# Kernel of two pairs of transformer blocks: order of work at the edges of the feed-forward sublayers

## The chip, the cores and the metric

One program on one core of a Trainium2 chip. The metric is the device time of one execution in microseconds. A core has four engines that compute (TensorE, VectorE, ScalarE, GpSimdE) and a fifth, SyncE, that issues transfers here. The engines run side by side and wait for each other by semaphores. In the trace they are PE (matrix multiplications; PEld for its weight loads), DVE, ACT, POOL and SP.

## The reference

256 tokens of width 1024 pass two layers of a first block and two layers of a second. A layer has three sublayers: feed-forward, mixer, feed-forward. The first block's sublayers read a condition (shift, scale, gate); the second block's take a norm of the result too.

```python
# first block, one layer
hn = _modulate(_rms_norm(h, norm_g[l, 0]), sh1, sc1)      # xn * (1 + scale) + shift
h = h + 0.5 * g1[:, None, :] * _swiglu(hn, ffn1_w_in[l], ffn1_w_out[l])
...                                                        # mixer: four kinds side by side, h = h + g2 * (mixed @ w_out)
hn = _modulate(_rms_norm(h, norm_g[l, 2]), sh3, sc3)
h = h + 0.5 * g3[:, None, :] * _swiglu(hn, ffn2_w_in[l], ffn2_w_out[l])

# second block
h = rms_norm(x, gn[0])
x = x + 0.5 * rms_norm(swiglu(h, w_ffn1_gate[l], w_ffn1_up[l], w_ffn1_down[l]), gn[1])

def _swiglu(x, w_in, w_out):
    gate, up = jnp.split(x @ w_in, 2, axis=-1)
    return (jax.nn.silu(gate) * up) @ w_out                # width 2816
```

## The kernel before

The twelve sublayers are numbered n = 0 to 11; n = 1, 4, 7, 10 are mixers and the other eight are feed-forward. Tokens are in two blocks of 128, a = 0 and 1. `h` holds the running sum in fp32. Every fp32 product is made of three multiplications: an operand is split into a high part, which ScalarE makes by a copy to a shorter format, and a low part, which VectorE makes by subtracting the high part from the original; low x high, high x low and high x high are added up in PSUM. `tok3` (lines 539 to 541) is this triple.

Weights come in units of 1 MB through three buffers: SyncE loads `raw`, ScalarE's `hi` (line 1049) makes `whi`, VectorE's `lo` (line 1507) makes `wlo`. Unit k can be loaded once unit k-3 has its low part. A feed-forward sublayer works through the 2816 hidden columns in eleven groups of 256. A group is two gate/up units (each half of the 1024 input columns) and one down unit. `k0` and `k0 + 1` are the sublayer's first two units.

At a boundary between sublayers the work on a token block a is a chain. VectorE adds the result to h (`residual`, lines 1526 and 1527), or, after sublayers of the second block, ScalarE squares the result first (line 1068) and VectorE scales by its norm. ScalarE squares h (line 1057), VectorE finds the inverse root (`norm_root`, lines 1422 to 1427) and scales h into `xs`, half by half (`scale_x`: lines 1568 and 1569 with norm_g and shift for n < 6, line 1572 after that). TensorE turns each half into PSUM banks 6 and 7 (`turn_x`, line 588), ScalarE copies it to `xh` (`upper_x`, line 1074) and VectorE subtracts to `xl` (`lower_x`, line 1578). In VectorE's order (`boundary`) block 0 comes first, then block 1's residual, then the low part of unit k0 + 1, then block 1.

TensorE's order at a feed-forward entry is written out in `ffn`: both halves of block 0 turned, 12 multiplications with unit k0, block 1's first half turned, 12 with unit k0 + 1, block 1's second half turned, four multiplications that zero the accumulators, then 24 multiplications for block 1. The groups follow. At the first one TensorE waits for the low part of unit k0 + 2 and for `h32`, the product of VectorE (lines 1652 and 1654). ScalarE makes the high part of that unit after its last `upper_x`.

At the end of the sublayer the last group's hidden values of both blocks are turned together into bank 6 (line 611), copied (line 1147) and subtracted (line 1659) as one tile of 512 columns, and lie in `xh` and `xl` from then on. All orders are program order on each engine; no scheduler moves anything.

## Time and profile before

| | us |
|---|---|
| median of 3 runs | 2605.33 (2604.96 to 2612.98) |
| the profiled execution | 2607.96 |
| its span in the profile | 2606.1 |
| TensorE busy | 2312.9 (89%) |
| VectorE busy | 1640.0 (63%) |
| ScalarE busy | 1082.2 (42%) |
| GpSimdE busy | 117.8 (5%) |
| mean granted TensorE clock | 0.941 |

Times in the rows are microseconds from the span's start. A row of the timeline has start, duration, engine, line and operation, what is written and read, and how many were merged; the bracket is how long the engine was idle before it and what ended that. Matrix multiplications are pipelined, so the difference of two starts is what one costs, not its own duration. In a view by stretches every engine has its busy time and its count, then come TensorE's granted clock, the DMA engines' busy share and what they moved in GB/s. The clock is 1.00 for 2.4 GHz and 0.50 for 1.2 GHz.

### The profile page before, as it was taken

To read this page: it belongs to the slowest core of one execution; us is meant where nothing else is said; L and a number is where in the kernel's file an instruction comes from. 1 tells how busy PE (TensorE), PEld (TensorE's weight loads), DVE (VectorE), ACT (ScalarE), POOL (GpSimd) and SP (SyncE) were. 2 spreads that over 40 slices of the span, in tenths; PEclk is the share of its full clock that TensorE was granted. 3 is DMA by queue.
4 is the path that set the end of the run, shared out by engine and by line. 5 is a ranking of instruction groups with operands and counts; after the bars stand their busy time and mean duration, and the time that the engine had idled before them with its cause. 6 is when DMAs were issued, how large, how long until landed. Compare 5 with 4: busy or idle time off the path is not lost.

```text
span 2606.1 us, 31632 instructions
## 1 busy us (share of the span) xinstructions
PE 2312.9 (89%) x11730; PEld 1941.2 (74%) x11740; DVE 1640.0 (63%) x1933; ACT 1082.2 (42%) x1246; POOL 117.8 (5%) x176
## 2 busy tenths in 40 slices
PE   1999799999899799899899787789989978957998
PEld 0787786787687686688788687668868868946887
DVE  6786875776776784655655566565565565646555
ACT  2434454343343363434343454434434335434443
POOL 1000033000000023000000000000000000000000
PEclk9999999999999998999999898789989989968999
DMA  7796552685586553456455442335546544323553
GB/s 241 269 314 199 194 170 81 242 284 192 203 280 220 166 197 97 152 187 194 161 191 182 136 121 80 113 129 194 188 134 195 191 145 130 117 61 115 185 185 113
DMA packets 321186, 452.75 MB, mean 174 GB/s; under 512 B 32470, under 2 KB 269896, under 8 KB 320072
## 3 DMA queue, kind: packets, MB, share of 16 engines
q1 hardware_dynamic: 314224, 439.43, 51.6%
q0 software_dynamic: 2816, 9.51, 1.1%
q10 hardware_dynamic: 4056, 2.58, 0.4%
q8 instruction: 59, 0.97, 0.2%
q14 instruction: 31, 0.25, 0.0%
HBM read 450.43 MB, written 1.05 MB: 173 GB/s over the span
## 4 chain that ended last, share of the span: by engine, by line
PE 78%; DVE 13%; ACT 4%; issue 2%; POOL 1%; DMA 1%; ACTq 1%; DVEq 0%; SPq 0%
PE ps L539 19%; PE ps L541 19%; PE ps L540 19%; PE ps L532 4%; PE ps L533 4%; PE ps L534 4%; PE ps L917 2%; PE ps L611 1%; DVE wlo L1507 1%; PE ps L756 1%; POOL nrm L2082 1%; PE ps L588 1%; DMA arena<-in_ada_w_dram 1%; PE ps L704 1%; PE ps L569 1%
## 5 line engine op out<-in xcount | busy, mean ns | idle before, releaser
L1507 DVE TENSOR_TENSOR wlo<-raw,whi 128x2048 fp32r<-128x2048 f32 (+1 forms) x348 | 791.7, 2278 | 439.8 <-ACT whi L1049 439.6
L1049 ACT ACTIVATE whi<-raw 128x2048 fp32r<-128x2048 f32 x346 | 659.6, 1909 | 275.2 <-PE ps L541 247.6
L539 PE MATMUL ps<-whi,xl 128*128 128x512 f32 x1600 | 657.8, 411 | 19.4 <-DVE xl L1866 10.5
L540 PE MATMUL ps<-wlo,xh 128*128 128x512 f32 x1600 | 635.3, 397 | 0.0
L541 PE MATMUL ps<-whi,xh 128*128 128x512 f32 x1600 | 634.7, 397 | 0.0
L539 PEld LDWEIGHTS ps<-whi,xl 128*128 128x128 f32 x1600 | 308.4, 193 | 91.1 <-issue 13.9
L541 PEld LDWEIGHTS ps<-whi,xh 128*128 128x128 f32 x1600 | 307.6, 192 | 67.4
L540 PEld LDWEIGHTS ps<-wlo,xh 128*128 128x128 f32 x1600 | 308.4, 193 | 65.4 <-issue 4.8
L532 PE MATMUL ps<-xl,whi 128*128 128x256 f32 x896 | 264.5, 295 | 16.5 <-DVE wlo L1507 15.2
L533 PE MATMUL ps<-xh,wlo 128*128 128x256 f32 x896 | 259.6, 290 | 0.0
L534 PE MATMUL ps<-xh,whi 128*128 128x256 f32 x896 | 259.1, 289 | 0.0
L539 PE MATMUL ps<-whi,hidl 128*128 128x512 f32 x640 | 252.5, 395 | 0.0
L540 PE MATMUL ps<-wlo,hidh 128*128 128x512 f32 x640 | 249.4, 390 | 0.0
L541 PE MATMUL ps<-whi,hidh 128*128 128x512 f32 x640 | 249.3, 390 | 0.0
L532 PEld LDWEIGHTS ps<-xl,whi 128*128 128x128 f32 x896 | 178.3, 199 | 20.6 <-DVE wlo L1507 16.0
L533 PEld LDWEIGHTS ps<-xh,wlo 128*128 128x128 f32 x896 | 178.3, 199 | 0.6 <-issue 0.5
L534 PEld LDWEIGHTS ps<-xh,whi 128*128 128x128 f32 x896 | 178.0, 199 | 0.0
L1142 ACT ACTIVATE sq<-ps 128x256 f32<-128x256 f32 x176 | 67.5, 384 | 246.8 <-PE ps L541 246.8
L1637 DVE SCALAR_TENSOR_TENSOR arena<-arena,condT 128x1024 f32<-128x1024 f32 x120 | 154.5, 1288 | 23.3 <-DMA arena<-in_ada_w_dram 21.8
L1150 ACT ACTIVATE hidh<-ps 128x512 fp32r<-128x512 f32 x80 | 47.9, 599 | 283.0 <-PE ps L611 283.0
L1662 DVE TENSOR_TENSOR hidl<-ps,hidh 128x512 fp32r<-128x512 f32 x80 | 55.3, 691 | 140.9 <-ACT hidh L1150 140.9
L540 PEld LDWEIGHTS ps<-wlo,hidh 128*128 128x128 f32 x640 | 120.3, 188 | 25.9 <-issue 1.4
(332 smaller groups left out, 2340.3 us busy)
## 6 DMA issues: line engine op xcount, KB each, us to landing
raw<-in_ffn_w_in_dram SPq DMA_DIRECT2D x176, 512.0 KB
arena<-in_ada_w_dram SPq DMA_DIRECT2D x128, 512.0 KB, 5.7
raw<-in_w_in_dram SPq DMA_DIRECT2D x54, 1024.0 KB
raw<-in_ffn_w_out_dram SPq DMA_DIRECT2D x44, 1024.0 KB
raw<-in_w_ffn_gate_dram SPq DMA_DIRECT2D x88, 512.0 KB
raw<-in_w_ffn_up_dram SPq DMA_DIRECT2D x88, 512.0 KB
raw<-in_w_ffn_down_dram SPq DMA_DIRECT2D x44, 1024.0 KB
raw<-in_w_out_dram SPq DMA_DIRECT2D x16, 1024.0 KB
```

The source lines that it names most:

```text
L532: pe.matmul(o, wh, al, start=start, stop=False, **kw)
L533: pe.matmul(o, wl, ah, start=False, stop=False, **kw)
L534: return pe.matmul(o, wh, ah, start=False, stop=stop, **kw)
L539: pe.matmul(o, al, wh, start=start, stop=False, **kw)
L540: pe.matmul(o, ah, wl, start=False, stop=False, **kw)
L541: return pe.matmul(o, ah, wh, start=False, stop=stop, **kw)
L917: pe.matmul(ps[:, PVB, ch * S:ch * S + S], diag[d % RING], ypad[:, ch, tap:tap + S], start=(tap == 0), stop=(tap == CONVK - 1)).then_inc(d ...
L1049: act.activation(whi[:, k % 3, :], raw[:, k % 3, :], ACT.Copy).then_inc(hi_done, 1)
L1142: act.activation(sig[:, a, :], ps[:, a, 0:256], ACT.Sigmoid).then_inc(sig_ready, 1)
L1507: tt(a[0], a[1], a[2].bitcast(F32), ALU.subtract).then_inc(lo_done, 1)
L1637: stt(seg, adam[:, at, :], scalar, seg, ALU.mult, ALU.add).then_inc(adam_used, 1)
L1662: tt(hidl[:, :, :].rearrange("p f t -> p (f t)"), ps[:, HT, :], hidh[:, :, :].bitcast(F32).rearrange("p f t -> p (f t)"), ALU.subtract).th ...
```

## The change

Four edits.
1. The last group's hidden values are turned, copied and subtracted by token block, block 0 into bank 6 and block 1 into bank 7 (`turn_last`, `upper_last`, `lower_last`), with semaphores of their own. The last down unit of block 0 needs block 0's part only. ScalarE's high part of the next sublayer's first unit comes between its two copies, VectorE's low part between its two subtractions. Bank 7 also carries the modulation's sums, so TensorE waits for the reads of these.
2. For n < 6 h is multiplied with norm_g (times 1 + scale) ahead of the inverse root (`gained`); behind it one operation multiplies with the root and adds the shift. For the first half of each block `gained` is issued ahead of the root, for the second between the two scalings.
3. The first use of x by TensorE is split (`gate_up_first`): eight multiplications that read `xh` alone are issued when it is there, the four with `xl` later.
4. The turns of x are spread: the second half of block 0 after the first eight multiplications, block 1's first half after unit k0 + 1's 12, its second half after eight of block 1.

```diff
+                def gate_up_first(k, a, half, part):
+
+                    wh, wl = as4(whi, k % 3), as4(wlo, k % 3)
+                    t = slice(a * P, a * P + P)
+                    pe.wait_ge((xh_ready, x_ready)[part], 4 * n + 2 * a + half + 1)
+                    for q in range(4):
+                        kc = 4 * half + q
+                        if part == 0:
+                            pe.matmul(ps[:, a, :], xh[:, kc, t], wl[:, q, :], start=(kc == 0), stop=False)
+                            ins = pe.matmul(ps[:, a, :], xh[:, kc, t], wh[:, q, :], start=False, stop=False)
+                        else:
+                            ins = pe.matmul(ps[:, a, :], xl[:, kc, t], wh[:, q, :], start=False, stop=(kc == KC - 1))
+                    return ins
+
+                def turn_last(a):
+
+                    pe.wait_ge(h32_ready, 2 * (g0 + GROUPS - 1) + a + 1)
+                    for f in range(2):
+                        ins = pe.transpose(ps[:, HT + a, f * P:f * P + P],
+                                           hid32[:, a, f * P:f * P + P], ident[:, :])
+                    ins.then_inc(tail_turned, 1)
 
...
                 turn_x(n, 0, 0)
+                split_ready(L, k0)
+                gate_up_first(k0, 0, 0, 0)
                 turn_x(n, 0, 1)
-                split_ready(L, k0)
-                gate_up(k0, 0, 0, True)
+                gate_up_first(k0, 0, 0, 1)
+                split_ready(L, k0 + 1)
+                gate_up_first(k0 + 1, 0, 1, 0)
+                gate_up_first(k0 + 1, 0, 1, 1).then_inc(gu_ready, 1)
                 turn_x(n, 1, 0)
-                split_ready(L, k0 + 1)
-                gate_up(k0 + 1, 0, 1, True).then_inc(gu_ready, 1)
-                turn_x(n, 1, 1)
                 for b in range(4):
                     pe.matmul(ps[:, ACC + b, :], zerow[:, 0:P], zerow[:, :], start=True, stop=True,
                               skip_group_check=True)
-                gate_up(k0, 1, 0, True).then_inc(unit_used, 1)
-                gate_up(k0 + 1, 1, 1, True).then_inc(unit_used, 1)
+                gate_up_first(k0, 1, 0, 0)
+                turn_x(n, 1, 1)
+                gate_up_first(k0, 1, 0, 1).then_inc(unit_used, 1)
+                gate_up_first(k0 + 1, 1, 1, 0)
+                gate_up_first(k0 + 1, 1, 1, 1).then_inc(unit_used, 1)
...
                 k += 7
-                down(k, 0)
-                turn_hid(GROUPS - 1)
-                down(k, 1, (0,))
+                down(k, 0, (0,))
+                turn_last(0)
+                down(k, 0, (1,))
+                if m:
+                    pe.wait_ge(mod_read, SUMS[m] + 6)
+                if n == 0:
+                    pe.wait_ge(gate0_read, 2)
+                turn_last(1)
                 split_ready(L, k + 1)
-                pe.wait_ge(hid_ready, g0 + GROUPS)
+                pe.wait_ge(tail_hid, 2 * L.ffn(j) + 1)
                 down(k + 1, 0, last=True).then_inc(acc_done, 1)
-                down(k, 1, (1,)).then_inc(unit_used, 1)
+                down(k, 1).then_inc(unit_used, 1)
+                pe.wait_ge(tail_hid, 2 * L.ffn(j) + 2)
                 down(k + 1, 1, last=True).then_inc(unit_used, 1)
...
+                def upper_last(a):
+                    act.wait_ge(tail_turned, 2 * L.ffn(j) + a + 1)
+                    act.activation(lasth[:, 2 * a:2 * a + 2, :],
+                                   ps[:, HT + a, 0:S].rearrange("p (c t) -> p c t", c=2),
+                                   ACT.Copy).then_inc(tail_hidh, 1)
 
...
                 sigmoid(g + 2, 1, k + 6)
+                upper_last(0)
                 if n < SUBS - 1:
                     hi(L, k + 9)
-                upper(g + 2)
+                upper_last(1)
...
+            def gained(n, a, f):
+
+                c = slice(512 * f, 512 * f + 512)
+                return tt(xs[:, a, c], h[:, a, c], gain[:, c], ALU.mult)
+
             def scale_x(n, a, f):
 
                 o = xs[:, a, 512 * f:512 * f + 512]
                 c = slice(512 * f, 512 * f + 512)
                 r = rstat[:, a, 1:2]
                 if n < 6:
-                    st(stt(o, h[:, a, c], r, gain[:, c], ALU.mult, ALU.mult))
-                    tt(o, o, shift[:, c], ALU.add).then_inc(xs_ready, 1)
+                    if f:
+                        st(gained(n, a, f))
+                    stt(o, o, r, shift[:, c], ALU.mult, ALU.add).then_inc(xs_ready, 1)
...
-                norm_root(n, 0)
                 if n < 6:
                     dve.wait_ge(mod_read, SUMS[n] + 6)
+                    gained(n, 0, 0)
                 else:
                     dve.wait_ge(gate_loaded, 16 * (n - 5))
+                norm_root(n, 0)
                 scale_x(n, 0, 0)
                 scale_x(n, 0, 1)
                 lower_x(n, 0, 0)
                 lower_x(n, 0, 1)
                 finish(n - 1, 1)
                 lo(L, k0 + 1)
+                if n < 6:
+                    gained(n, 1, 0)
                 norm_root(n, 1)
                 scale_x(n, 1, 0)
...
+                def lower_last(a):
+                    dve.wait_ge(tail_hidh, 2 * L.ffn(j) + a + 1)
+                    c = slice(2 * a, 2 * a + 2)
+                    tt(lastl[:, c, :], ps[:, HT + a, 0:S].rearrange("p (c t) -> p c t", c=2),
+                       lasth[:, c, :].bitcast(F32), ALU.subtract).then_inc(tail_hid, 1)
 
...
-                lower(g + 2)
+                lower_last(0)
                 if n < SUBS - 1:
                     lo(L, k + 9)
+                lower_last(1)
```

Three places where instructions move, all around the entry of sublayer 2 or the end of a feed-forward sublayer. A row is line, operation, what is written and read, shape, and the semaphores waited for; "..." leaves out rows that repeat.

TensorE at a feed-forward entry, before. `ps<-ident,u` is a turn of x, `whi` and `wlo` are the weight unit's parts; the last row is the first group's first multiplication:

```order
L588 MATMUL ps<-ident,u 128x128 [waits xs_ready]
L588 MATMUL ps<-ident,u 128x128 [waits xs_ready]
...
L539 MATMUL ps<-whi,xl 128x512 [waits x_ready,lo_done]
...
L588 MATMUL ps<-ident,u 128x128 [waits x_ready,xs_ready]
...
L539 MATMUL ps<-whi,xl 128x512 [waits x_ready,lo_done]
...
L588 MATMUL ps<-ident,u 128x128 [waits x_ready,xs_ready]
...
L638 MATMUL ps<-zerow 128x512 x4
L539 MATMUL ps<-whi,xl 128x512 [waits x_ready]
...
L539 MATMUL ps<-whi,xl 128x512 [waits x_ready]
...
L539 MATMUL ps<-whi,xl 128x512 [waits h32_ready]
```

and now:

```order
L589 MATMUL ps<-ident,u 128x128 [waits xs_ready]
...
L614 MATMUL ps<-wlo,xh 128x512 [waits xh_ready,lo_done]
...
L589 MATMUL ps<-ident,u 128x128 [waits xs_ready]
...
L617 MATMUL ps<-whi,xl 128x512 [waits x_ready]
...
L614 MATMUL ps<-wlo,xh 128x512 [waits xh_ready,lo_done]
...
L589 MATMUL ps<-ident,u 128x128 [waits x_ready,xs_ready]
...
L660 MATMUL ps<-zerow 128x512 x4
L614 MATMUL ps<-wlo,xh 128x512 [waits xh_ready]
...
L589 MATMUL ps<-ident,u 128x128 [waits x_ready,xs_ready]
...
L617 MATMUL ps<-whi,xl 128x512 [waits x_ready]
...
L614 MATMUL ps<-wlo,xh 128x512 [waits xh_ready]
...
L540 MATMUL ps<-whi,xl 128x512 [waits h32_ready]
```

The second turn moved behind the first unit's eight multiplications with xh, the third behind the second unit's 12, and behind the fourth stand 16 multiplications where 24 stood.

TensorE at the end of a feed-forward sublayer, before. The rows of line 539 that read `hidl` belong to the last but one group's down unit, those that read `xl` to the last group's:

```order
L539 MATMUL ps<-whi,hidl 128x512 [waits hid_ready,lo_done]
...
L611 MATMUL ps<-ident,u 128x128 [waits h32_ready]
L611 MATMUL ps<-ident,u 128x128 x3
L539 MATMUL ps<-whi,hidl 128x512
...
L539 MATMUL ps<-whi,xl 128x512 [waits hid_ready,lo_done]
...
L539 MATMUL ps<-whi,hidl 128x512
...
L539 MATMUL ps<-whi,xl 128x512
```

and now:

```order
L540 MATMUL ps<-whi,hidl 128x512 [waits hid_ready,lo_done]
...
L624 MATMUL ps<-ident,u 128x128 [waits h32_ready]
L624 MATMUL ps<-ident,u 128x128
L540 MATMUL ps<-whi,hidl 128x512
...
L624 MATMUL ps<-ident,u 128x128 [waits h32_ready,mod_read]
...
L540 MATMUL ps<-whi,xl 128x512 [waits tail_hid,lo_done]
...
L540 MATMUL ps<-whi,hidl 128x512
...
L540 MATMUL ps<-whi,xl 128x512 [waits tail_hid]
```

Four turns at one place became two and two, and block 0's last product has six multiplications fewer ahead of it; they stand behind it.

VectorE at the entry of sublayer 2, before. `rstat` is the root, `u` holds xs, `wlo` is the low part of unit k0 + 1:

```order
L1527 TENSOR_TENSOR h<-h,sq 128x512 [waits dve_step]
L1422 SCALAR_TENSOR_TENSOR rstat<-ssq 128x1 [waits sq_ready]
...
L1568 SCALAR_TENSOR_TENSOR u<-h,rstat,gain 128x512 [waits mod_read,dve_step]
L1569 TENSOR_TENSOR u<-u,shift 128x512 [waits dve_step]
L1568 SCALAR_TENSOR_TENSOR u<-h,rstat,gain 128x512
L1569 TENSOR_TENSOR u<-u,shift 128x512 [waits dve_step]
L1578 TENSOR_TENSOR xl<-ps,xh 128x4x128 [waits xh_ready] x2
...
L1527 TENSOR_TENSOR h<-h,sq 128x512 [waits dve_step]
L1507 TENSOR_TENSOR wlo<-raw,whi 128x2048 [waits hi_done]
L1422 SCALAR_TENSOR_TENSOR rstat<-ssq 128x1 [waits sq_ready]
```

and now:

```order
L1561 TENSOR_TENSOR h<-h,sq 128x512 [waits dve_step]
L1599 TENSOR_TENSOR u<-h,gain 128x512 [waits mod_read]
L1456 SCALAR_TENSOR_TENSOR rstat<-ssq 128x1 [waits sq_ready]
...
L1609 SCALAR_TENSOR_TENSOR u<-u,rstat,shift 128x512 [waits dve_step]
L1599 TENSOR_TENSOR u<-h,gain 128x512
L1609 SCALAR_TENSOR_TENSOR u<-u,rstat,shift 128x512 [waits dve_step]
L1618 TENSOR_TENSOR xl<-ps,xh 128x4x128 [waits xh_ready] x2
...
L1561 TENSOR_TENSOR h<-h,sq 128x512 [waits dve_step]
L1541 TENSOR_TENSOR wlo<-raw,whi 128x2048 [waits hi_done]
L1599 TENSOR_TENSOR u<-h,gain 128x512
L1456 SCALAR_TENSOR_TENSOR rstat<-ssq 128x1 [waits sq_ready]
```

One product with the gain moved ahead of each root; behind the root one operation is left for the first half, and two for the second as before.

## Rows read from the trace of the kernel before

**Rows 1.** Page; stretch: busy (count) of PE, PEld, DVE, ACT, POOL, clock, DMA, GB/s
```profile
PE 2312.9 (89%) x11730; PEld 1941.2 (74%) x11740; DVE 1640.0 (63%) x1933; ACT 1082.2 (42%) x1246; POOL 117.8 (5%) x176
...
690.00:860.00 170.00, 169.89 (x757) 138.03 (x756) 119.53 (x108) 69.42 (x64) 3.16 (x2) 1.00 0.75 256
```

**Rows 2.** Timeline (start, duration, engine, line), the last group of sublayer 2
```profile
644.03 0.39 PE L539 MATMUL ps<-whi,hidl 128*128 128x512 f32 x1
...
644.51 1.91 ACT L1049 ACTIVATE whi<-raw 128x2048 fp32r<-128x2048 f32 x1
...
646.75 0.60 PE L611 MATMUL ps<-ident,u 128*128 128x128 f32 x4
...
648.62 2.28 DVE L1507 TENSOR_TENSOR wlo<-raw,whi 128x2048 fp32r<-128x2048 f32 x1
...
648.86 0.47 PE L539 MATMUL ps<-whi,xl 128*128 128x512 f32 x1
...
651.90 0.69 DVE L1526 TENSOR_TENSOR sq<-ps,gate 128x512 f32<-128x512 f32 x1 [0.99 <-PE ps L541]
```

**Rows 3.** Timeline, the entry of sublayer 3, up to its first group
```profile
655.44 0.16 DVE L1422 SCALAR_TENSOR_TENSOR rstat<-ssq 128x1 f32<-128x1 f32 x1 [0.79 <-ACT sq L1057]
...
657.23 0.75 DVE L1568 SCALAR_TENSOR_TENSOR u<-h,rstat,gain 128x512 f32<-128x512 f32 x1
...
658.76 0.33 PE L588 MATMUL ps<-ident,u 128*128 128x128 f32 x1 [2.82 <-DVE u L1569]
...
661.93 0.69 DVE L1578 TENSOR_TENSOR xl<-ps,xh 128x512 fp32r<-128x512 f32 x1 [1.16 <-ACT xh L1074]
...
665.19 2.29 DVE L1507 TENSOR_TENSOR wlo<-raw,whi 128x2048 fp32r<-128x2048 f32 x1
...
670.71 0.69 PE L588 MATMUL ps<-ident,u 128*128 128x128 f32 x2 [5.80 <-DVE u L1569]
...
676.74 0.60 PE L588 MATMUL ps<-ident,u 128*128 128x128 f32 x4
...
677.08 0.64 PEld L638 LDWEIGHTS ps<-zerow 128*128 128x128 bf16 x4
...
677.38 0.60 ACT L1074 ACTIVATE xh<-ps 128x512 fp32r<-128x512 f32 x1 [4.92 <-PE ps L588]
...
677.86 0.58 PE L539 MATMUL ps<-whi,xl 128*128 128x512 f32 x1
...
677.88 1.91 ACT L1049 ACTIVATE whi<-raw 128x2048 fp32r<-128x2048 f32 x1
...
682.48 0.42 DVE L1654 TENSOR_TENSOR u<-sq,ps 128x256 f32<-128x256 f32 x1
```

**Rows 4.** Timeline, TensorE at the first turn of sublayer 2
```profile
451.69 1.12 PE L588 MATMUL ps<-ident,u 128*128 128x128 f32 x4 [3.31 <-DVE u L1569]
```

**Rows 5.** Timeline, sublayer 9: first square, first turn, second lowering
```profile
1917.28 0.60 ACT L1068 ACTIVATE sq<-ps 128x512 f32<-128x512 f32 x1 [3.91 <-PE ps L541]
...
1926.04 1.97 PE L588 MATMUL ps<-ident,u 128*128 128x128 f32 x8 [4.72 <-DVE u L1572]
...
1928.67 0.69 DVE L1578 TENSOR_TENSOR xl<-ps,xh 128x512 fp32r<-128x512 f32 x1 [0.16 <-ACT xh L1074]
```

**Rows 6.** Timeline, sublayer 11: first turn, both lowerings
```profile
2399.20 1.32 PE L588 MATMUL ps<-ident,u 128*128 128x128 f32 x8 [3.37 <-DVE u L1572]
...
2400.53 1.35 DVE L1578 TENSOR_TENSOR xl<-ps,xh 128x512 fp32r<-128x512 f32 x2 [0.71 <-ACT xh L1074]
```

**Rows 7.** Columns as in rows 1, entries of 3, 11, 6; timeline, turn of 6
```profile
660.00:663.00 3.00, 2.85 (x9) 2.45 (x10) 1.84 (x4) 0.65 (x2) 0.00 (x0) 0.50 0.00 0
2401.00:2406.00 5.00, 4.63 (x11) 3.70 (x12) 4.65 (x15) 0.35 (x2) 0.00 (x0) 0.50 0.00 0
1256.00:1259.00 3.00, 2.90 (x12) 2.05 (x12) 2.93 (x6) 0.72 (x2) 0.00 (x0) 1.00 0.00 0
...
1253.74 0.99 PE L588 MATMUL ps<-ident,u 128*128 128x128 f32 x5 [2.09 <-DVE u L1572]
```

More of the change, by code:

```diff
@@ L214, in program @@
         ht_done, hidh_ready, hid_ready = sem("ht_done"), sem("hidh_ready"), sem("hid_ready")
+        tail_turned, tail_hidh, tail_hid = sem("tail_turned"), sem("tail_hidh"), sem("tail_hid")
         diag_ready, diag_used = sem("diag_ready"), sem("diag_used")
@@ L592, in ffn, with gate_up @@
             def ffn(L, n, j, k0):
-                g0, m = L.ffn(j) * GROUPS, (n + 1 if n < 5 else 0)
-                def gate_up(k, a, half, first=False):
+                g0, h0, m = L.ffn(j) * GROUPS, L.ffn(j) * (GROUPS - 1), (n + 1 if n < 5 else 0)
+                def gate_up(k, a, half):
                     wh, wl = as4(whi, k % 3), as4(wlo, k % 3)
                     t = slice(a * P, a * P + P)
-                    if first:
-                        pe.wait_ge(x_ready, 4 * n + 2 * a + half + 1)
                     for q in range(4):
@@ L621, in down @@
                         if last:
-                            ah, al = lasth[:, 2 * f + a, :], lastl[:, 2 * f + a, :]
+                            ah, al = lasth[:, 2 * a + f, :], lastl[:, 2 * a + f, :]
                         for b in range(2):
@@ L662, in group @@
                     split_ready(L, k + 4, ki)
-                    pe.wait_ge(hid_ready, g0 + g + 1)
+                    pe.wait_ge(hid_ready, h0 + g + 1)
                     if last:
@@ L1134, in ffn @@
             def ffn(L, n, j, k0):
-                g0, m = L.ffn(j) * GROUPS, (n + 1 if n < 5 else 0)
+                g0, h0, m = L.ffn(j) * GROUPS, L.ffn(j) * (GROUPS - 1), (n + 1 if n < 5 else 0)
                 def sigmoid(g, a, k=0, i=0):
@@ L1144, in upper @@
                 def upper(g):
-                    act.wait_ge(ht_done, g0 + g + 1)
-                    if isinstance(g, int) and g == GROUPS - 1:
-                        act.activation(lasth, ps[:, HT, :].rearrange("p (c t) -> p c t", c=4),
-                                       ACT.Copy).then_inc(hidh_ready, 1)
-                    else:
-                        act.activation(hidh[:, :, :].rearrange("p f t -> p (f t)"), ps[:, HT, :],
-                                       ACT.Copy).then_inc(hidh_ready, 1)
+                    act.wait_ge(ht_done, h0 + g + 1)
+                    act.activation(hidh[:, :, :].rearrange("p f t -> p (f t)"), ps[:, HT, :],
+                                   ACT.Copy).then_inc(hidh_ready, 1)
+                def upper_last(a):
[3 more added lines that the diff above has]
+                                   ACT.Copy).then_inc(tail_hidh, 1)
                 hi(L, k0 + 2)
@@ L1618, in first @@
                 dve.wait_ge(mod_read, 4)
+                st(gained(0, 0, 0))
                 scale_x(0, 0, 0)
                 scale_x(0, 0, 1)
+                st(gained(0, 1, 0))
                 scale_x(0, 1, 0)
@@ L1646, in ffn @@
             def ffn(L, n, j, k0):
-                g0, m = L.ffn(j) * GROUPS, (n + 1 if n < 5 else 0)
+                g0, h0, m = L.ffn(j) * GROUPS, L.ffn(j) * (GROUPS - 1), (n + 1 if n < 5 else 0)
                 def product(g, a):
@@ L1656, in lower @@
                 def lower(g):
-                    dve.wait_ge(hidh_ready, g0 + g + 1)
-                    if isinstance(g, int) and g == GROUPS - 1:
-                        tt(lastl, ps[:, HT, :].rearrange("p (c t) -> p c t", c=4), lasth.bitcast(F32),
-                           ALU.subtract).then_inc(hid_ready, 1)
-                    else:
-                        tt(hidl[:, :, :].rearrange("p f t -> p (f t)"), ps[:, HT, :],
-                           hidh[:, :, :].bitcast(F32).rearrange("p f t -> p (f t)"), ALU.subtract).then_inc(hid_ready, 1)
+                    dve.wait_ge(hidh_ready, h0 + g + 1)
+                    tt(hidl[:, :, :].rearrange("p f t -> p (f t)"), ps[:, HT, :],
+                       hidh[:, :, :].bitcast(F32).rearrange("p f t -> p (f t)"), ALU.subtract).then_inc(hid_ready, 1)
+                def lower_last(a):
[3 more added lines that the diff above has]
+                       lasth[:, c, :].bitcast(F32), ALU.subtract).then_inc(tail_hid, 1)
                 lo(L, k0 + 2)
```

## The prediction

> **What bounds the kernel.** I read the page's first part, then the wait lists and a search of TensorE's idle time over the span, then the timeline around the sublayer boundaries. The reader is to see three things. First, TensorE is busy 89% of the span, and inside a feed-forward sublayer it is never idle: 169.89 of 170 us at full clock, VectorE 70% busy beside it [rows 1]. So nothing inside absorbs a delay or turns a gain into idle time: what the change does at a boundary is kept, whatever its sign. Second, at a boundary TensorE is idle twice. At the entry of sublayer 3 that is 2.82 us before the first turn of x and 5.80 us before the third, both ended by VectorE [rows 3]. Third, between these waits TensorE runs at half rate: granted 0.50, 11 multiplications of 512 columns in 4.63 us (0.42 to 0.43 each), against 1.00 and 0.225 us each in the interior, 170 us by 757 instructions [rows 1, 7]. I number sublayers 0 to 11; 0, 2, 3, 5, 6, 8, 9, 11 are feed-forward, and 1 to 5 have the shift and the scaled norm_g.
>
> **Last group by token block.** Before, a block's last products follow 12 multiplications, four turns, 6 more multiplications, then the wait for `lastl`; first issue at 648.86, VectorE's residual at 651.90 [rows 2]. Now six multiplications from 644.03 (1.36 us), two turns, six, two turns, and the last 12 start at 647.15 if block 0's high and low parts are there. They are: turn issued at 645.4, ScalarE's copy from 645.9 (0.64 us behind the turns, as at 676.74, less for half of them), 0.4 us, VectorE 0.4 us, done 646.7. So block 0's sums are complete 1.7 us earlier, 650.2. For these half-size copies and subtractions no row stands; 0.60 and 0.69 of the whole ones bound them above, half of that below; I take 0.4, as the 256-column product in rows 3 takes 0.42. ScalarE's split of the next unit (1.91 us) moves from 644.51 behind the first copy, 646.2 to 648.1; VectorE's lower part of it then runs 648.1 to 650.4, and the second block's subtraction ends at 650.7. VectorE is thus free at 650.7, not 650.2: where it reads the sums itself (sublayers 1, 3, 4, 6) the gain is 1.2 us. Where ScalarE squares the sums first (7, 9, 10; it waits for TensorE [rows 5]) it is the full 1.7. At the program's end the second block's own sums come only 0.3 earlier, and VectorE 0.8.
>
> **norm_g ahead of the root.** The first product h x gain (0.69) goes into VectorE's 0.79 us wait for the squares [rows 3]: free; if the squares were there already it would cost up to 0.69. Behind the root one operation of 0.75 remains of 0.75 + 0.69 (the scaling at 657.23, and a two-operand operation as at 651.90): first turn 0.7 us earlier, in sublayers 1 to 5. For block 1 VectorE doesn't wait, so the product only changes places: nothing gained.
>
> **First turn, in sum:** 1.9 earlier in 1, 3, 4; 0.7 in 2, 5; 1.2 in 6; 1.7 in 7, 9, 10; 0 in 8, 11. In the mixers (1, 4, 7, 10) PE's order is untouched and every later wait is VectorE's chain, which moves along: -(1.9+1.9+1.7+1.7) = -7.2 us. End: -0.8.
>
> **High part first.** Eight multiplications now stand between the turns of x's halves. They start when ScalarE has copied the first half: turn + 0.69 + 0.60 + 0.05 = 1.34 us. At 0.23 they take 1.8, at 0.43 3.4 (3.2 if the clock returns within). Then turn 2, 0.69 (1.1 at half rate) to ScalarE, 0.63 to VectorE. So the second lowering starts 4.5 us after the first turn at full clock, 6.3 at half. Before it was 3.2 us in 3 [rows 3], which I take for 2 and 5 too, 2.6 in 9 [rows 5] and 2.0 in 11 (1.35 us for both, from 2400.53) [rows 6]. Queued behind this lowering in VectorE are block 1's residual, the lower half of the second gate/up unit, the root and block 1's scaling: all of that moves.
>
> **Second turn later.** Before, TensorE resumed when root and scaling were done, 670.71, 3.23 us after the split of the second unit ended (665.19 + 2.29) [rows 3]. Now the next 12 multiplications need only that split: 3.2 us off the wait, 2.5 where no shift is added (from 6 on). Resume, against before:
> 2 and 5, half rate: -3.2 - 0.7 + (6.3 - 3.2) = -0.8 each;
> 3, full: -3.2 - 1.9 + (4.5 - 3.2) = -3.8;
> 6, full: -2.5 - 1.2 + (4.5 - 2.0) = -1.2;
> 9, half: -2.5 - 1.7 + (6.3 - 2.6) = -0.5;
> 8 and 11, half: -2.5 + (6.3 - 2.0) = +1.8 each.
> Sum -3.5. Which clock I take: the idle time before the first turn, 2.82 us in 3 and 3.31 to 4.72 in 2, 9 and 11, left it at half rate [rows 3 to 7]; in 6, after 2.09, it stayed full [rows 7]. In 3 and 6 that idle time shrinks to about 1.4 and 1.2.
>
> **What comes late next.** This is the largest term. Before, the fourth turn (676.74) was issued ahead of the zeroing and 24 multiplications: 0.34 + 0.78 + 24 x 0.225 = 6.5 us to the first group. The chain behind it is turn, ScalarE's copy (677.38), the split of the third unit in ScalarE's queue (677.88), its lower part, the product, which ends at 682.90 [rows 3]: 6.16 us, hidden with 0.3 to spare. Now only 16 multiplications follow the fourth turn: 0.34 + 3.6 = 3.94 us. The chain is as long, since ScalarE and VectorE still have copy, split, lower and product in that order. With 0.05 us for the signal TensorE waits 6.21 - 3.94 = 2.25 us ahead of the first group. Against it stands that one turn now runs at full instead of half rate (0.4, of which the multiplications in its place take back 0.2 or all). Net 2.0 in each of seven: +14. Its bounds: 1.8 (sublayer 3, all 12 of the resume at half rate) and 2.3. Loads follow the lower parts and move with TensorE; DMA at 0.75 in the interior [rows 1] leaves room.
> Sublayer 0: eight multiplications slip into a wait that is not in my rows' pattern and the same late chain is paid: 0, bounds -2 and +2.
> No multiplication is added; waits on banks 6 and 7 (the modulation's copies) are for work that ScalarE has long done: 0, and at most one copy, 0.6, in the five sublayers that have them.
>
> **Sum:** -7.2 - 0.8 - 3.5 + 14 + 0 = +2.5 us on the profiled execution's 2607.96 (its span 2606.1 and 1.9 around it). That execution lies 2.6 above the median of 2605.33; on the median: 2607.8.
>
> On the clock: in sublayer 6 the trace shows 2.09 us idle and still 1.00 [rows 7], in 3 a longer one and 0.50. [...]
>
> **Rivals.**
> 1. Slower: the new stall of 2.25 us, just above the 2.09 that kept the clock and below the 2.82 that did not, drops TensorE to half rate at the first group. Ten to twelve multiplications at 0.43 for 0.23 cost 2.0 to 2.4. It decides from an idle time between 2.1 and 2.8. Seven times 2.0: +16.5, 2621.8. Against: full work stands on both sides of the stall, where at a boundary there are only turns. Chance 0.16.
> 2. Half rate at every first half: +6.1, 2611.4. Chance 0.17.
> 3. Full rate at every first half, since TensorE starts sooner after its turns: 2, 5, 8, 9, 11 gain 1.8 each, -9: sum -6.5, 2598.8. Against: 8 and 11 wait 3.4 us as before. Chance 0.10.
> 4. The late chain hides after all (a split of the third unit that ran ahead of the copy, or a slower TensorE in front of it): -14, sum -11.5, 2593.8. For it: half-rate multiplications behind the fourth turn would cover it. Against: by then TensorE has worked through 20 multiplications without a wait, and both queues run in program order. Chance 0.12.
> My forecast 0.45.
>
> A measurement of this kernel tells 0.3% (7.8 us) from no change. Faster: rival 4 and a quarter of 3: 0.15. Slower: rival 1, a third of 2, a tenth of mine: 0.26. Same: 0.59. Range: from 2597, between rivals 4 and 3, to 2621, near rival 1.
>
> **What would show it.** In the new trace: TensorE's last 12 for block 0 about 1.7 us after the first two turns, with no wait; VectorE's residual 1.2 us sooner; first turn of 3 idle-free except for 1.4 us. The third turn without idle time and the idle time moved to the high-part multiplication of the second unit, waiting for VectorE's lower split. An idle time of 2 to 2.3 us at the first group's first multiplication in seven sublayers, ended by the product: the step I would be most wrong without. Second lowering 4.5 or 6.3 us after the first turn, as the clock is. I am wrong if that idle time is absent, if it is over 3 us, or if the interior shows idle time at all.

## The result and the profile after

The kernel after takes 2623.8 us (median of 7 runs, 2616.8 to 2631.8), the kernel before on the same chip 2606.1: ratio 1.0064 [1.0053, 1.0075], 17.7 us slower. The forecast was 2607.8, range 2597 to 2621. The profiled executions differ by 17.1 (spans 2623.2 and 2606.1).

The page of the kernel after, first part, and its interior of sublayer 3 (stretch, busy and count of PE, PEld, DVE, ACT, POOL, clock, DMA, GB/s), which answer to [rows 1]:

```profile
PE 2316.9 (88%) x11730; PEld 1940.6 (74%) x11740; DVE 1639.2 (62%) x1941; ACT 1082.8 (41%) x1254; POOL 115.1 (4%) x176
...
690.00:860.00 170.00, 170.00 (x759) 138.26 (x758) 119.35 (x107) 69.53 (x65) 3.16 (x2) 1.00 0.77 263
```

The same number of matrix instructions, and an interior as full and as fast as before: the time was lost at boundaries alone.

The end of sublayer 2 and the first turn of sublayer 3 after (timeline: start, duration, engine, line, operation), which answer to [rows 2] and the head of [rows 3]:

```profile
651.30 0.39 ACT L1182 ACTIVATE xh<-ps 128x256 fp32r<-128x256 f32 x1 [1.20 <-PE ps L624]
...
651.72 0.43 DVE L1709 TENSOR_TENSOR xl<-ps,xh 128x256 fp32r<-128x256 f32 x1 [0.70 <-ACT xh L1182]
...
655.74 0.42 DVE L1709 TENSOR_TENSOR xl<-ps,xh 128x256 fp32r<-128x256 f32 x1
...
656.07 0.68 DVE L1560 TENSOR_TENSOR sq<-ps,gate 128x512 f32<-128x512 f32 x1
...
658.72 0.68 DVE L1599 TENSOR_TENSOR u<-h,gain 128x512 f32<-128x512 f32 x1
...
661.38 0.75 DVE L1609 SCALAR_TENSOR_TENSOR u<-u,rstat,shift 128x512 f32<-128x512 f32 x1
...
662.19 0.66 PE L589 MATMUL ps<-ident,u 128*128 128x128 f32 x4 [1.09 <-DVE u L1609]
```

Copy and subtraction of half size take 0.39 and 0.43 (I took 0.4 each), VectorE goes straight from the subtraction to the residual, the product with norm_g lies ahead of the root, and from the residual to the first turn it is 6.12 us instead of 6.86. TensorE is idle for 1.09 us there, not 2.82. This half of the change does what it should.

The entry of sublayer 3 after, same columns, which answers to the rest of [rows 3]. L614 and L615 are the multiplications that read `xh`, L617 those with `xl`, L589 the turns:

```profile
663.63 0.47 PE L614 MATMUL ps<-wlo,xh 128*128 128x512 f32 x1 [0.78 <-ACT xh L1105]
...
666.67 1.05 PE L589 MATMUL ps<-ident,u 128*128 128x128 f32 x4
...
668.39 0.69 DVE L1618 TENSOR_TENSOR xl<-ps,xh 128x512 fp32r<-128x512 f32 x1 [4.18 <-ACT xh L1105]
...
671.65 2.28 DVE L1541 TENSOR_TENSOR wlo<-raw,whi 128x2048 fp32r<-128x2048 f32 x1
...
673.99 0.80 PE L614 MATMUL ps<-wlo,xh 128*128 128x512 f32 x1 [5.33 <-DVE wlo L1541]
...
678.64 0.60 PE L589 MATMUL ps<-ident,u 128*128 128x128 f32 x4
...
681.88 0.60 PE L589 MATMUL ps<-ident,u 128*128 128x128 f32 x4
...
682.52 0.60 ACT L1105 ACTIVATE xh<-ps 128x512 fp32r<-128x512 f32 x1 [2.64 <-PE ps L589]
...
683.01 1.91 ACT L1080 ACTIVATE whi<-raw 128x2048 fp32r<-128x2048 f32 x1
...
684.95 2.29 DVE L1541 TENSOR_TENSOR wlo<-raw,whi 128x2048 fp32r<-128x2048 f32 x1 [1.11 <-ACT whi L1080]
...
687.61 0.42 DVE L1699 TENSOR_TENSOR u<-sq,ps 128x256 f32<-128x256 f32 x1
...
688.09 0.50 PE L540 MATMUL ps<-whi,xl 128*128 128x512 f32 x1 [1.89 <-DVE u L1699]
```

Read it from the bottom. The first group's first multiplication waits 1.89 us for the product, and the product ends a chain that began with the fourth turn at 681.88: turn, copy, split, lower part, product, without a pause in it. Further up, the second turn is issued at 666.67, so VectorE waits 4.18 us for its second lowering (6.20 us after the first turn), while TensorE's next 12 multiplications need the lower split queued behind that lowering and wait 5.33 us.

What that comes to over the whole program, in the groups of the kernel after by line (busy, mean ns | idle time before them, what ended it):

```profile
L540 PE MATMUL ps<-whi,xl 128*128 128x512 f32 x1472 | 598.3, 406 | 25.6 <-DVE u L1699 15.1 <-DVE xl L1914 10.5
...
L614 PE MATMUL ps<-wlo,xh 128*128 128x512 f32 x128 | 65.7, 513 | 49.1 <-DVE wlo L1541 42.9 <-ACT xh L1105 6.2
...
L589 PE MATMUL ps<-ident,u 128*128 128x128 f32 x192 | 34.8, 317 | 53.6 <-DVE u L1612 39.9 <-DVE u L1609 13.7
```

And the turns' own group before:

```profile
L588 PE MATMUL ps<-ident,u 128*128 128x128 f32 x192 | 39.6, 349 | 100.8 <-DVE u L1572 62.8 <-DVE u L1569 37.9
```

47.2 us of idle time ahead of turns went away; 49.1 came at L614 and 15.1 at the group's first multiplication, eight times 1.89. I looked next for the clock behind these eight waits. Stretches of 3.5 us in the kernel after, each beginning 0 to 0.5 us behind the first multiplication after the wait (the fourth, at 1080.50, 1.1 us behind it, where the clock falls), columns as in rows 1:

```profile
83.75:87.25 3.50, 3.50 (x9) 2.72 (x10) 3.47 (x4) 2.34 (x2) 0.00 (x0) 0.53 0.82 249
479.75:483.25 3.50, 3.50 (x9) 2.74 (x10) 3.47 (x4) 2.12 (x2) 0.00 (x0) 0.52 0.89 253
688.10:691.60 3.50, 3.50 (x15) 2.91 (x16) 3.47 (x4) 2.13 (x2) 0.00 (x0) 1.00 0.71 228
1080.50:1084.00 3.50, 3.50 (x10) 2.76 (x9) 3.50 (x2) 1.04 (x1) 0.00 (x0) 0.52 0.90 281
1282.30:1285.80 3.50, 3.50 (x15) 2.90 (x16) 3.46 (x4) 2.11 (x2) 0.00 (x0) 1.00 0.85 255
1756.25:1759.75 3.50, 3.50 (x9) 2.78 (x10) 3.47 (x4) 2.02 (x2) 0.00 (x0) 0.53 0.83 260
1964.50:1968.00 3.50, 3.50 (x10) 2.70 (x10) 3.50 (x3) 1.63 (x1) 0.00 (x0) 0.53 0.88 293
2439.00:2442.50 3.50, 3.50 (x10) 2.67 (x10) 3.47 (x4) 1.86 (x2) 0.00 (x0) 0.52 0.92 285
```

In six of eight the granted clock is near 0.50 and 9 or 10 multiplications are issued; in sublayers 3 and 6 it stays at 1.00 and 15 are. The loss is counted best from the first multiplication after the wait to the turn that follows 24 of them, here in sublayers 3 and 2:

```profile
688.09 0.50 PE L540 MATMUL ps<-whi,xl 128*128 128x512 f32 x1 [1.89 <-DVE u L1699]
...
693.66 0.60 PE L632 MATMUL ps<-ident,u 128*128 128x128 f32 x4
```
```profile
479.73 0.67 PE L540 MATMUL ps<-whi,xl 128*128 128x512 f32 x1 [1.89 <-DVE u L1699]
...
486.88 0.49 PE L632 MATMUL ps<-ident,u 128*128 128x128 f32 x3
```

It is 5.58 us in 3 and 6, where the clock held, and 7.15 to 7.20 in the other six: 1.6 us lost at each, 9.7 in all.

### The profile page after: what moved, and what is told of

Read it like the earlier page. It is cut to its first block, busy times and chain, and to the rows that moved or that the text cites. A ratio compares the mean times of both kernels' runs of the same rounds, so it can differ in the third digit from the quotient of the medians.

```text
span 2623.2 us, 31648 instructions
## 1 busy us (share of the span) xinstructions
PE 2316.9 (88%) x11730; PEld 1940.6 (74%) x11740; DVE 1639.2 (62%) x1941; ACT 1082.8 (41%) x1254; POOL 115.1 (4%) x176
## 4 chain that ended last, share of the span: by engine, by line
PE 77%; DVE 13%; ACT 4%; issue 2%; POOL 1%; DMA 1%; ACTq 1%; DVEq 0%; SPq 0%
PE ps L540 18%; PE ps L542 17%; PE ps L541 17%; PE ps L533 4%; PE ps L534 4%; PE ps L535 4%; DVE wlo L1541 2%; PE ps L948 2%; PE ps L614 1%; PE ps L632 1%; PE ps L787 1%; PE ps L615 1%; POOL nrm L2130 1%; ACT whi L1080 1%; DMA arena<-in_ada_w_dram 1%
## 5 line engine op out<-in xcount | busy, mean ns | idle before, releaser
L540 PE MATMUL ps<-whi,xl 128*128 128x512 f32 x1472 | 598.3, 406 | 25.6 <-DVE u L1699 15.1
L541 PE MATMUL ps<-wlo,xh 128*128 128x512 f32 x1472 | 579.7, 394 | 0.0
L542 PE MATMUL ps<-whi,xh 128*128 128x512 f32 x1472 | 579.7, 394 | 0.0
L540 PEld LDWEIGHTS ps<-whi,xl 128*128 128x128 f32 x1472 | 280.1, 190 | 89.7 <-DVE u L1699 18.5
L542 PEld LDWEIGHTS ps<-whi,xh 128*128 128x128 f32 x1472 | 279.9, 190 | 61.1
L541 PEld LDWEIGHTS ps<-wlo,xh 128*128 128x128 f32 x1472 | 280.2, 190 | 60.0 <-issue 4.8
L540 PEld LDWEIGHTS ps<-whi,hidl 128*128 128x128 f32 x640 | 120.2, 188 | 25.9 <-issue 1.4
```

What stands on the lines that cost most here:

```text
L540: pe.matmul(o, al, wh, start=start, stop=False, **kw)
L541: pe.matmul(o, ah, wl, start=False, stop=False, **kw)
L542: return pe.matmul(o, ah, wh, start=False, stop=stop, **kw)
```

## The experiments

Each is compared with the kernel before on its own chip. "Against after" below is the quotient of the two ratios to before, times 2606.

**The fourth turn early (`fourth_early`), the second turn early (`second_early`), both.** Edits of the kernel after; `both_early` makes both and leaves only the third turn late.

```diff
                 turn_x(n, 0, 0)
+                turn_x(n, 0, 1)              # second_early
                 split_ready(L, k0)
                 gate_up_first(k0, 0, 0, 0)
-                turn_x(n, 0, 1)
...
+                turn_x(n, 1, 1)              # fourth_early
                 gate_up_first(k0, 1, 0, 0)
-                turn_x(n, 1, 1)
```

> The changed kernel with one line moved: block 1's second turn stands right behind the zeroing instead of behind eight multiplications of block 1. Theory (late chain and clock): the 1.89 us wait ahead of the first group goes in all eight sublayers (to 0.4 us at most, since 24 multiplications, 5.4 us, then stand behind the turn and the chain is 6.2 us), and with it the six stretches at half rate behind it, 1.5 us each. Together 8 x 1.5 to 1.9 + 6 x 1.5 = 21 to 24 us faster than the changed kernel, so 4 to 7 us faster than the kernel before (ratio about 0.998). Rival (the wait is a symptom; TensorE would be late for another reason, for instance the third unit's split itself): the wait moves elsewhere and the time stays within 5 us of the changed kernel, ratio 1.005 to 1.006.

> The changed kernel with the turn of block 0's second half back in front of the first eight multiplications. The fourth turn stays late. Theory: the second lowering comes 2.0 to 3.2 us after the first turn instead of 4.6 to 7.2 (1.9 to 4.2 us earlier in seven sublayers, 25 us in sum), and block 1's residual, the split of the second unit and the third turn all move with it; 25 us faster than the changed kernel, 8 us faster than before (ratio 0.997). The 1.89 us wait ahead of the first group stays in all eight. Rival (the eight multiplications only fill time that VectorE needs anyway): under 8 us faster than the changed kernel.

> Both turns moved as in the two other kernels: second turn ahead of the first eight multiplications, fourth right behind the zeroing. Only the third turn stays behind the second unit's 12. Theory: both gains add, 45 us faster than the changed kernel and about 28 us faster than before (ratio 0.989). Rival: they overlap, since either leaves TensorE waiting for VectorE; then no better than the better of the two, ratio 0.996 to 0.998.

Measured: 2596.5, 0.9960 [0.9947, 0.9973]; 2597.0, 0.9957 [0.9944, 0.9969]; 2569.8, 0.9854 [0.9839, 0.9868]. Against after -27, -28 and -54: the two late turns cost the same, and the costs add up. Groups of `both_early`:

```profile
L540 PE MATMUL ps<-whi,xl 128*128 128x512 f32 x1472 | 594.6, 404 | 11.6 <-DVE xl L1914 10.5 <-DVE u L1699 0.3
...
L614 PE MATMUL ps<-wlo,xh 128*128 128x512 f32 x128 | 62.0, 485 | 22.3 <-DVE wlo L1541 22.1
```

The wait for the product falls from 15.1 to 0.3 and that at L614 from 49.1 to 22.3. These 42 us of idle time explain most of the 54. The clock behind the first group's start holds in all eight sublayers (24 multiplications in 5.58 to 5.62 us), which is the 9.7 us from above; the last 3 us are not accounted for. All three came out better than expected (21 to 24, 25 and 45 us).

In `second_early` the wait of 1.89 us stays in all eight sublayers, and the clock fell behind it in seven: also in 3 and 6, where it had held in the kernel after, and not in sublayer 0, where it had fallen.

**The wait filled (`late_filled`).** The kernel after, with eight multiplications by zero added onto the output banks ahead of the first group; this separates the wait from the clock behind it.

```diff
                 gate_up_first(k0 + 1, 1, 1, 1).then_inc(unit_used, 1)
+                for b in range(8):
+                    pe.matmul(ps[:, ACC + b % 4, :], zerow[:, 0:P], zerow[:, :], start=False, stop=False,
+                              skip_group_check=True)
```

> The changed kernel with eight more multiplications by zero (512 columns, added onto the accumulators, result unchanged) ahead of the first group, that is in the 1.89 us wait; each takes about 0.2 us, 1.7 together. Theory (the wait's own time and the clock behind it are two separate costs): the wait's time stays, but TensorE is not idle, the clock doesn't fall there, and the six half-rate stretches of 1.5 us go: 9 us faster than the changed kernel, 8 to 9 slower than before (ratio 1.003). Rival (the clock falls for an earlier idle time, not for this one): no faster than the changed kernel, ratio 1.006 or a little above.

Measured: 2614.2, 1.0026 [1.0017, 1.0035], -10 against after, although the product comes no sooner. The traced execution took 2622.4, 8 over this median, so I read from it the stretches behind the zeros and not its whole. The zeros of sublayer 3 in the timeline, and then, for the six sublayers whose clock fell before, the window behind the zeros (stretch, PE busy and count, clock, DMA, GB/s):

```profile
681.79 1.90 PE L668 MATMUL ps<-zerow 128*128 128x512 bf16 x8
...
683.84 0.50 PE L540 MATMUL ps<-whi,xl 128*128 128x512 f32 x1
```
```profile
83.96:87.46 3.50, 3.50 (x15) 1.00 0.83 224
478.70:482.20 3.50, 3.50 (x15) 1.00 0.80 227
...
1079.59:1083.09 3.50, 3.50 (x15) 1.00 0.80 247
...
1755.22:1758.72 3.50, 3.50 (x15) 1.00 0.79 245
1962.71:1966.21 3.50, 3.50 (x15) 1.00 0.83 254
2437.76:2441.26 3.50, 3.50 (x15) 1.00 0.80 238
```

The six places that were at 0.52 are at 1.00, and 15 multiplications stand where 9 or 10 stood. The 24 multiplications behind the zeros take 5.58 to 5.62 us in all eight sublayers. So the fall of the clock is caused by the idle time and costs 10 us by itself, beside the 15 of the wait; the run (-10) and the count in the trace of the kernel after (9.7) agree.

**The parts apart.** `entry_only`: the kernel before with parts 3 and 4 of the change alone, TensorE's new order. `tail_and_gain`: the kernel after with the old order. `tail_only`: the last group by token block alone (part 1). `gain_only`: norm_g ahead of the root alone (part 2).

```diff
# tail_and_gain, from the kernel after; entry_only is the reverse, from the kernel before
                 turn_x(n, 0, 0)
+                turn_x(n, 0, 1)
                 split_ready(L, k0)
-                gate_up_first(k0, 0, 0, 0)
-                turn_x(n, 0, 1)
-                gate_up_first(k0, 0, 0, 1)
+                gate_up(k0, 0, 0, True)
+                turn_x(n, 1, 0)
...
# gain_only, from the kernel before
-                    st(stt(o, h[:, a, c], r, gain[:, c], ALU.mult, ALU.mult))
-                    tt(o, o, shift[:, c], ALU.add).then_inc(xs_ready, 1)
+                    if f:
+                        st(gained(n, a, f))
+                    stt(o, o, r, shift[:, c], ALU.mult, ALU.add).then_inc(xs_ready, 1)
# tail_only, from the kernel before
-                down(k, 0)
-                turn_hid(GROUPS - 1)
-                down(k, 1, (0,))
+                down(k, 0, (0,))
+                turn_last(0)
+                down(k, 0, (1,))
```

> The kernel before with TensorE's new order at the feed-forward entries alone (high part first, second, third and fourth turn later); the last group and norm_g as before. Theory (all of the loss is in this order and the clock it brings, the other two edits gain what was forecast for them): 30 us slower than before, the changed kernel's 17 plus the 14 that the other two gain (ratio 1.012). Rival (one of the other edits costs time too, for instance the tail's later split of the next unit): then this one is only about as slow as the changed kernel, ratio 1.006 to 1.007.

> The changed kernel with TensorE's entry order put back as it was before; the last group by token block and norm_g ahead of the root stay. Theory: the first turn comes 0.7 to 1.9 us earlier in ten of eleven entries as read, 15.4 us from them (three times 1.9, two times 0.7, 1.2, three times 1.7, and 0.8 at the end make 14.2); ratio 0.9945. Rival (the gains are lost again where TensorE waits for the third turn): under 6 us, ratio above 0.9975.

> The kernel before with only the last group turned, copied and subtracted by token block. Theory: 1.2 us in sublayers 1, 3, 4 and 6, 1.7 in 7, 9 and 10, 0.8 at the end: 10.7 us faster, ratio 0.996. Rival (the split of the next unit, which moves behind the first copy, takes the gain back): ratio 0.998 or more.

> The kernel before with only norm_g multiplied ahead of the root. Theory: 0.72 us at the first turn of sublayers 1 to 5, 3.6 us in all, ratio 0.9986. Rival (the product ahead of the root delays the root): no gain or a loss of up to 3.5 us, ratio 1.000 to 1.001.

Measured: `entry_only` 2636.6, 1.0121 [1.0107, 1.0136]; `tail_and_gain` 2594.2, 0.9954 [0.9943, 0.9966]; `tail_only` 2591.2, 0.9943 [0.9931, 0.9956]; `gain_only` 2602.1, 0.9984 [0.9975, 0.9992]. In us +31.5, -12, -15, -4. The terms listed in the expectation of `tail_and_gain` make 14.2, not 15.4. The whole loss, and more, is in TensorE's order. `entry_only` has the same wait in all eight sublayers, here in sublayer 3:

```profile
685.45 0.50 PE L539 MATMUL ps<-whi,xl 128*128 128x512 f32 x1 [1.89 <-DVE u L1670]
```

Behind that wait the clock fell in three of eight (6, 8 and 11) in its trace. `tail_only` gained 15 us for the 11 expected. Tail and norm_g together bring less than the sum of the two, 12 for 19; the intervals of the three, 3 us each way, leave a part of that open, and I did not look into it.

**The turns where they were, high part first (`turns_as_before`).** The kernel after with turns 1 and 2 together and turns 3 and 4 at their old places, only the multiplications still split by part.

```diff
                 turn_x(n, 0, 0)
+                turn_x(n, 0, 1)
                 split_ready(L, k0)
                 gate_up_first(k0, 0, 0, 0)
-                turn_x(n, 0, 1)
                 gate_up_first(k0, 0, 0, 1)
+                turn_x(n, 1, 0)
                 split_ready(L, k0 + 1)
                 gate_up_first(k0 + 1, 0, 1, 0)
                 gate_up_first(k0 + 1, 0, 1, 1).then_inc(gu_ready, 1)
-                turn_x(n, 1, 0)
+                turn_x(n, 1, 1)
...
                 gate_up_first(k0, 1, 0, 0)
-                turn_x(n, 1, 1)
```

> The changed kernel with all four turns where they stood in the kernel before; the high part is still multiplied first, the last group and norm_g as changed. Theory: multiplying the high part first by itself only fills time before the third turn, so this is the time of the kernel with the other two edits alone, 12 to 14 us faster than before (ratio 0.995); what lies between it and the version with second and fourth turn early (0.985) is the third turn's move, about 25 us. Rival (the split is what pays in that version): 20 us or more faster than before, ratio 0.992 or less.

Measured: 2588.2, 0.9923 [0.9910, 0.9936]: 20 us faster than before, at the rival's bound and not the 12 to 14 of the theory. Against `tail_and_gain` high part first brings 8 us with no turn moved (on another chip, so by the ratios), and the late third turn that `both_early` adds (its fourth turn also stands behind the four zeroing multiplications) brings another 18. I had put nearly all on the third turn.

**Filling the other wait (`resume_filled`, `both_fill4`, `both_fill8`).** Ten zero multiplications into bank 0 ahead of unit k0 + 1 in the kernel after, and 4 or 8 in `both_early`.

```diff
                 gate_up_first(k0, 0, 0, 1)
+                for _ in range(10):          # 4, 8
+                    pe.matmul(ps[:, 0, :], zerow[:, 0:P], zerow[:, :], start=False, stop=False,
+                              skip_group_check=True)
```

> The changed kernel with ten multiplications by zero (added onto the open sum, result unchanged) in the 5.3 to 7.2 us wait for the second unit's lower part, in all feed-forward entries. They take 2.2 us at full and 4.3 at half rate, so they end before the wait does. Theory (the clock that falls in this wait is a cost of its own): the 12 multiplications behind it run at 0.23 instead of 0.40 us, 2 us in each of seven sublayers; 12 to 15 us faster than the changed kernel, ratio to before 1.001 to 1.002. Rival (TensorE would wait for block 1's scaling or for the late chain instead): under 5 us, ratio 1.005.

> The version with second and fourth turn early (0.9854 of before) with four multiplications by zero in its wait for the second unit's lower part (1.7 to 4.2 us). Theory: part of the half-rate time behind the wait goes, 3 to 7 us faster than that version, ratio 0.983 to 0.984. Rival (what remains idle still lets the clock fall): no change.

> The same with eight multiplications by zero, 1.8 us at full and 3.4 at half rate. Theory: 8 to 12 us faster than the version without, ratio 0.981 to 0.982, less what they delay in the two entries whose wait is under 2.5 us. Rival (they cost TensorE's time and the third turn waits for block 1's scaling instead): no faster, ratio 0.985 or more.

Measured: 2617.8, 1.0039 [1.0026, 1.0052]; 2564.1, 0.9833 [0.9821, 0.9846]; 2564.0, 0.9829 [0.9816, 0.9841]. `resume_filled` is 6.5 us under after, where the theory said 12 to 15 and the rival under 5. Its TensorE in sublayer 3:

```profile
665.47 2.33 PE L656 MATMUL ps<-zerow 128*128 128x512 bf16 x10
670.98 0.80 PE L614 MATMUL ps<-wlo,xh 128*128 128x512 f32 x1 [3.18 <-DVE wlo L1544]
671.57 0.63 PE L615 MATMUL ps<-whi,xh 128*128 128x512 f32 x1
```

The ten ran at once, 3.18 us of idle time were left, and the multiplications behind it are 0.43 us apart: half rate again. So it is in six of seven sublayers; only in 5, where 2.40 us of idle time were left, they ran at full rate. Two half-rate stretches fewer behind the 1.86 to 1.89 us waits (four of eight for six) account for 3.2 us of the gain. With eight zeros in `both_early`, whose wait is 3.50 us there, no wait is left at this place in sublayer 3. Its group over the program:

```profile
L614 PE MATMUL ps<-wlo,xh 128*128 128x512 f32 x128 | 59.2, 463 | 8.9 <-DVE wlo L1544 8.7
```

Idle time 8.9 for 22.3, mean 463 ns for 485. `both_fill8` is the fastest kernel of this study, 44 us under the kernel before; 4 zeros do as well within the intervals, though they stop short of the wait's end (1.8 to 3.3 us stay idle in seven sublayers): TensorE then runs at full rate up to the first group in four of the seven (5, 6, 9 and 11), against two in `both_early` (2 and 5). The 5 and 7 us that they gain over `both_early` are at the edge of what two chips' ratios can tell (0.9833 and 0.9829 against 0.9854). For 8 zeros that is less than the 8 to 12 expected. By the traces the time from the first turn to the first group shrinks by 8.8 us in 3, 6, 9 and 11 together, stays in 2, 5 and 8, and grows by 2.0 in sublayer 0.

## Why the prediction was wrong

Take T, the first turn of a feed-forward sublayer, and G, the first multiplication of its first group. I forecast the time from T to G, summed over eight sublayers, to grow by 16.7 us, and measured 24.0 (1.4, 2.8, 1.1, 1.9, 4.0, 4.5, 3.7, 4.6 for 0, 2, 3, 5, 6, 8, 9, 11). From G to the next T (the end, behind 11) I forecast -12.8 (the tail's and norm_g's gains) and found -2.3. The mixers, from their first turn to the next T, gave -3.4 for -1.4, and the start -1.2 for 0. Together +17.1 for +2.5.

- **What comes late next: right in its mechanism, a little over in its size.** The fourth turn's chain ends last, at the place, by the releaser and with the queue order forecast: 1.89 us for 2.25. It also appears in sublayer 0, which I had put at 0 with bounds of 2 us either way; that sublayer gave +1.4. Rival 4, that the chain hides, is out.
- **The step that failed is rival 1's, at chance 0.16.** I argued that full work on both sides of the wait would keep the clock. In six of eight sublayers it did not. Those falls lie behind G and ate the tail's gain: 10.5 us are missing between G and the next T, 10.2 of them in these six (1.5 to 1.9 each). In 3 and 6, where the clock held, the stretch shrank by 1.9 and 1.4 for 1.9 and 1.7 forecast. `late_filled` takes 10 us off by filling the wait. I had also made the case depend on a wait over 2.09 us, because that one kept the clock in sublayer 6 [rows 7]; 1.89 dropped it six times and kept it twice. One row in which the clock held was no bound. Over four kernels with this wait unfilled (1.86 to 1.89 us) the clock fell in 6, 7, 3 and 4 of eight places (after, `second_early`, `entry_only`, `resume_filled`); what decides stays open.
- **Which clock I take: wrong in 3 and 6.** I let the eight high-part multiplications run at full rate there, since less idle time was left before the first turn. That time did shrink, to 1.09 and 1.21, and still the clock fell in the stretch behind it. The kernel after, sublayers 3 and 6 (columns as for `late_filled`):

```profile
664.00:668.00 4.00, 4.00 (x14) 0.57 0.00 0
...
1258.00:1261.50 3.50, 3.45 (x8) 0.52 0.00 0
```

  The second lowering thus starts 6.20 and 6.19 us after the first turn, not 4.5: 1.7 us each. This is rival 2's content, which priced it at 1.8 each (2.5 and 3.6 make its +6.1). The kernel that the Trainium skill describes ("TensorE: Matmul & The Clock Gate", "HAM oscillation — how this bites in real kernels") starts every burst at half rate behind waits of about 3 to 5 us. That settles nothing for these two: their idle times were shorter, 1.09 and 1.21 us and 0.78 more ahead of the eight multiplications, and the clock fell all the same, 0.6 us into the work in 3 and 0.1 us in 6.
- **Second turn later: right in its mechanism, wrong where the clock was.** TensorE's resume, counted from T, moved by -0.1 in 2, 5 and by 0, 1.8, 1.2, 1.8 in 6, 8, 9, 11 and -1.9 in 3 by my terms; measured +0.8, -1.3, +1.8, +1.5, +1.1, +1.6 and -0.2. The misses are 3 and 6 with 1.7 each, +0.9 in 2 and -1.2 in 5 (its first half at full rate): 5.3 us for 2.7. The idle time ahead of the 12 multiplications grew from 33.7 us over seven sublayers to 42.9, which I had not worked out, and with it came the next point.
- **Behind the resume: a term I left out.** From the resume to G I forecast +2.0 in each of seven and measured 1.3 to 3.2, 17.2 in sum for 14, though the wait itself is 0.36 smaller. TensorE from the resume to G in 8 and 11, first before, then after, columns as for `late_filled`:

```profile
1735.34:1746.51 11.17, 11.11 (x47) 0.87 0.40 165
2411.14:2422.33 11.19, 11.13 (x46) 0.87 0.18 75
```
```profile
1741.76:1754.25 12.49, 12.44 (x47) 0.82 0.51 168
2424.30:2436.83 12.53, 12.47 (x47) 0.82 0.24 84
```

  The second pair ends where the new wait begins. From the first of these 47 instructions to the start of the last it is 12.1 us for 11.1 and 11.2, at a mean clock of 0.82 for 0.87: some 1.6 us more at half rate. The idle time ahead had grown from 4.33 to 7.24 us, but its length doesn't show as the cause: in `second_early`, behind 3.49 us in sublayer 9 and 3.67 in 11, the half rate took 6.0 and 5.2 us up to G, more than behind 7.24 in the kernel after (5.1 and 4.6). Why it lasts longer stays open. 2.6 in the point above, 3.3 in this one, and 1.4 in sublayer 0 are the 7.3 missing between T and G. Over everything, `second_early` shows what the late second turn costs: 28 us.
- **Last group, norm_g: right.** -7.2 - 0.8 in mixers and end and 6.2 within the sublayers forecast, 14.2; `tail_and_gain` measured 12, within its interval of 3. The parts alone came to 15 and 4 for 10.7 and 3.5.
- **Rival 3** (full rate everywhere) is out: of the seven first halves behind sublayer 0 only sublayer 5's ran at full rate (its second lowering came after 4.63 us).

The range ended at 2621 and the time is 2623.8: rival 1 and rival 2 are both largely true, and I had never added them. Forecast 2607.8 plus 9.7 for rival 1 at six places plus 3.4 for rival 2 is 2621; the longer half rate behind the resume and sublayer 0 bring 4.7 more, and the start and the mixers gave 3.2 back. That makes 2622.4, 1.4 short of the median; 0.8 of these are the kernel before, which took 2606.1 here and 2605.3 in the forecast. No experiment split these smaller terms further.

## What to carry to other kernels

On an engine that is full, moving a producer behind eight multiplications moves everything queued behind its consumer on the other engines; follow that whole chain to the next wait before moving it, and move only the one whose own input is late (here the third turn), not its neighbours. Price every new wait twice, for its idle time and for the clock behind it (here 1.9 and 1.6 us, the second in 20 of 32 places), and add the rivals that can be true together. Where a wait can't be removed, zero multiplications that reach to its end are the safe choice: they kept the clock at all eight places. Zeros that stopped short kept it behind them at one of seven places in `resume_filled` and at four of seven in `both_fill4`.

## What the runs showed of the hardware

- A TensorE wait of 1.89 us between two full stretches was followed by a granted clock near 0.50 in six cases (0.52 or 0.53 over 3.5 us; 1.2 GHz for 2.4) and by 1.00 in two, in one execution. The same place with the same wait fell in one kernel and held in another: sublayers 3 and 6 held in the kernel after and fell in `second_early`, sublayer 0 the other way round. The wait's length alone doesn't decide.
- The clock fell in the middle of work too: in sublayer 3 the first turn and two multiplications ran at full rate, and the rate halved at 664.2 with TensorE busy.
- bf16 zero multiplications issued every 0.22 us into the wait kept the clock at 1.00 behind them in `late_filled`, at all eight places; in sublayer 3 of `resume_filled` 2.33 us of them followed by 3.18 us idle did not.
- Copying 128x256 out of a bank takes ScalarE 0.39 us and subtracting it 0.43 on VectorE, for 0.60 and 0.69 at 512 columns: half the size is over 0.6 of the time.
